# Block 2, first layer: two modulation rows moved from the first attention pairs to the front of the key-value projection

## The reference

```python
mod_x = (jax.nn.silu(c) @ w_mod[i] + b_mod[i])[:, None, :]
mod_c = (jax.nn.silu(c_ctx) @ w_mod[i] + b_mod[i])[None, None, :]
sh1, sc1, ga1, sh2, sc2, ga2 = jnp.split(mod_x, 6, axis=-1)
...
hx = rmsnorm_2(x, g_pre_mix[i]) * (1.0 + sc1) + sh1
px = hx @ w_in[i]
...
mix_x = jnp.concatenate([attn_x, four_x, hy_x], axis=-1) @ w_out[i]
x = x + ga1 * rmsnorm_2(mix_x, g_post_mix[i])
```

## Time and profile before

| what | value |
|---|---|
| median of 3 runs | 1646.79 us (1645.38 to 1646.94) |
| the profiled execution | 1647.11 us, its span 1645.3 us |
| TensorE busy | 1591.5 us |
| VectorE (DVE) busy | 1107.7 us |
| ScalarE (ACT) busy | 833.4 us |
| granted TensorE clock, mean | 0.996 of full speed |
| loads from memory | 259.12 MB |

### The profile page before, as it was taken

How to read it: one execution, slowest core, us unless ns; L and a number is a source line. 1 busy time by engine, 2 the same in 40 slices (tenths; PEclk the granted TensorE clock), 3 DMA queues, 4 the chain that set the end, 5 groups by cost and what they waited for, 6 DMA issues and landing times. The chain is left out here.

```text
span 1645.3 us, 22529 instructions
## 1 busy us (share of the span) xinstructions
PE 1591.5 (97%) x8474; PEld 1277.2 (78%) x8474; DVE 1107.7 (67%) x1822; ACT 833.4 (51%) x1524; POOL 265.1 (16%) x321
## 2 busy tenths in 40 slices
PE   8999999999999999999999999999999998899998
PEld 7667888787677888878846788888788786678886
DVE  5686899556867998655775654445433577589974
ACT  5555667445656666442354543333421544566653
POOL 2000011810003112700000001101272000001163
PEclk9999999999999999999999999999999999999999
DMA  8555866555579654551197433333232342356652
GB/s 275 174 190 168 227 184 183 191 183 178 194 240 264 170 158 151 205 179 63 73 318 246 129 103 102 103 87 92 103 128 87 107 133 91 92 148 184 187 188 86
DMA packets 267277, 261.72 MB, mean 159 GB/s; under 512 B 8965, under 2 KB 208937, under 8 KB 266530
## 3 DMA queue, kind: packets, MB, share of 16 engines
q1 hardware_dynamic: 262994, 246.15, 48.7%
q0 software_dynamic: 3888, 13.81, 2.4%
q10 hardware_dynamic: 288, 0.33, 0.1%
HBM read 259.12 MB, written 1.13 MB: 158 GB/s over the span
## 5 line engine op out<-in xcount | busy, mean ns | idle before, releaser
L578 PE MATMUL psv<-hHL,wH 128*128 128x512 f32 (+1 forms) x1952 | 639.1, 390 | 2.9 <-DVE wL L1286 2.9
L1286 DVE TENSOR_TENSOR wL<-ring,wH 128x1024 fp32r<-128x1024 f32 (+2 forms) x364 | 450.8, 1241 | 234.9 <-ACT wH L1969 231.7
L1969 ACT ACTIVATE wH<-ring 128x1024 fp32r<-128x1024 f32 (+2 forms) x364 | 377.2, 1040 | 274.4 <-PE psv L578 265.9
L578 PE MATMUL psv<-hHL,wL 128*128 128x256 f32 (+1 forms) x1504 | 465.1, 309 | 0.0
L578 PEld LDWEIGHTS psv<-hHL,wH 128*128 128x128 f32 x1952 | 363.3, 188 | 86.6 <-DVE wL L1286 6.4
L578 PE MATMUL psv<-wH,hHL 128*128 128x512 f32 (+2 forms) x936 | 318.0, 389 | 10.7 <-DVE hHL L1553 4.7
L578 PEld LDWEIGHTS psv<-hHL,wL 128*128 128x128 f32 x1504 | 283.6, 189 | 15.7
L578 PE MATMUL pss<-wH,hHL 128*128 128x512 f32 (+3 forms) x808 | 272.0, 381 | 0.0
L578 PEld LDWEIGHTS psv<-wH,hHL 128*128 128x128 f32 x936 | 175.7, 189 | 53.3 <-DVE wL L1286 9.5
L578 PE MATMUL psv<-wL,hHL 128*128 128x512 f32 (+2 forms) x468 | 179.9, 384 | 0.0
L1101 POOL TENSOR_TENSOR W<-scr 128x256 f32<-128x256 f32 (+1 forms) x88 | 82.4, 937 | 582.3 <-ACT scr L2178 582.3
(11 more groups left out here) (270 smaller groups left out, 1602.0 us busy)
## 6 DMA issues: line engine op xcount, KB each, us to landing
ring<-in_w_up SPq DMA_DIRECT2D x176, 512.0 KB, 5.1
ring<-in_w_mod SPq DMA_DIRECT2D x96, 512.0 KB, 5.0
ring<-in_w_down SPq DMA_DIRECT2D x88, 512.0 KB, 4.2
ring<-in_w_in SPq DMA_DIRECT2D x52, 512.0 KB, 4.7
ring<-in_w_out SPq DMA_DIRECT2D x32, 512.0 KB, 4.8
ring<-in_w_in SPq DMA_DIRECT2D x8, 384.0 KB, 5.7
W<-gate_scratch POOLq DMA_DIRECT2D x3, 1024.0 KB, 5.0
ring<-in_w_in SPq DMA_DIRECT2D x8, 288.0 KB, 6.9
```

The costliest lines, as they stand in the source:

```text
L578: return pe.matmul(o, a, b, start=start, stop=stop, skip_group_check=True)
L1286: v.tensor_tensor(lo, raw, hi.bitcast(F32), ALU.subtract).then_inc(piece_split, told("piece_split", p))
L1969: return ac.activation(o, i, ACT.Copy)
```

## The change

Rows 1 and 2 of the second layer's modulation leave the table `pairs` and stand in a new entry `between`; the entry `heads`, empty before, goes. The other seven rows of the table are spread on pairs 0, 2, 3, 5, 6, 8 and 10. On TensorE and on DVE row 1 now comes behind the gate transpose and row 2 behind the second forward transform's step; in the ring the four chunks stand between the query chunks and the key-value chunks.

```diff
-        MOD2 = [{"start": [0], "heads": [], "pairs": {0: 1, 1: 2, 2: 3, 3: 4, 5: 5, 6: 6, 7: 7, 9: 9, 10: 11}, "ffn": [8], "end": [10]},
-                {"start": [], "heads": [], "pairs": {}, "ffn": [], "end": []}]
+        MOD2 = [{"start": [0], "between": [1, 2], "pairs": {0: 3, 2: 4, 3: 5, 5: 6, 6: 7, 8: 9, 10: 11}, "ffn": [8], "end": [10]},
+                {"start": [], "between": [], "pairs": {}, "ffn": [], "end": []}]
...
             add_cols(A["w_in_2"][l], 0, 512, ph, "q")
+            add_mod(1, MOD2[l]["between"])
             add_cols(A["w_in_2"][l], 512, 512, ph, "kvf")
             add_raw(A["w_fourier_2"][l], 0, FOW)
-            add_mod(1, MOD2[l]["heads"])
             add_mod(1, MOD2[l]["pairs"].values())
...
                 transposes("V", (ph, "gates"), [(rowc[:, :], slice(0, P))])
+                for c in MOD2[l]["between"][0:1]:
+                    modulation_row(1, c)
                 hyena_back(0)
                 if not last:
                     hyena_forward(1)
+                for c in MOD2[l]["between"][1:]:
+                    modulation_row(1, c)
                 project_split(range(4), [512] * nt + [256] * (4 - nt), (ph, "kvf"))
...
-                modulation(1, MOD2[l]["heads"])
...
                 take_rows(96, ph, "gates")
+                for c in MOD2[l]["between"][0:1]:
+                    modulation_row(1, c)
                 hyena_gate(0)
                 if not last:
                     hyena_products(1)
+                for c in MOD2[l]["between"][1:]:
+                    modulation_row(1, c)
                 splits_to(first_piece[ph, "kvf"] + 2, 0)
...
-                modulation(1, MOD2[l]["heads"])
```

## The result

The changed kernel takes **1653.55 us** (median of 4 runs, 1651.83 to 1654.99), the kernel before 1646.37 us beside it (4 runs, 1645.38 to 1646.94): ratio 1.0044, 95% interval 1.0033 to 1.0056. It is slower by more than 0.2%, and the time lies 1.25 us above the range of the prediction. A second measurement (12 runs of it, 32 of the kernel before) gave 1651.42 against 1646.24 us: ratio 1.0034, interval 1.0021 to 1.0046. The intervals overlap, from 1.0033 to 1.0046. By the second ratio the cost is 5.6 us, which puts the changed kernel at 1652.4 us, just above the range; so the sign of the result is firm, and its distance from the range is not.

What follows compares the result with a forecast made beforehand. TensorE, busy for 97% of the span, was taken as the bound. New idle 2.83 plus moved work 3.72 less 4.33 saved in attention gave +2.2 us on 1646.8: 1649.0 us, range 1646.8 to 1652.3.

Steps and rivals of the forecast that it cites:

- The look-ahead: Ahead of the key-value projection: DVE's low halves follow row 2's addition, PE idles 2.8 us, the projection starts 6.55 us later.
- The chunk in time: Ahead of the key-value projection: the weight chunk lands in 4.1 us, at 788.6, with 4.4 us in hand.
- Pair 1: In attention, without a row: 5.29 us instead of 6.80, with PE idle 3.14 us until ACT's exponentials are done.
- What the attention gives back: From pair 1's to pair 11's scores: 50.32 us becomes 45.99, a saving of 4.33 us.
- 2.83 + 3.72 - 4.33: New idle ahead of the projection plus moved row work less the attention's saving: +2.2 us.
- the clock falls in one of the new gaps: Rival: half clock after the projection's or pair 1's gap; 1650.7 us with one fall (chance 0.30), 1652.3 with two (0.08).
- one gap of 2.66 us: PE's wait in pair 1 of the kernel before: matmuls after it showed no clock fall.
- between 2.66 and 3.00 us: The idle time on PE from which the clock was taken to fall; the new gaps were 2.8 and 3.14 us.
- The price of one fall: Eight transposes and four score matmuls at 1.2 GHz after a gap: 1.65 us more, paid in full.
- late weights: Rival: the key-value chunk lands late, PE waits ahead of the projection; 1649.8 us, or 1652.8 with 1 MB more; chance 0.08.
- pair 1 like pair 4: Rival, in attention: pair 1 takes 3.48 us in place of 5.29, time 1647.2 us; chance 0.08.
- the untouched look-ahead: Rival: low halves still come ahead of the row, the projection's 2.83 us idle vanishes, time 1646.2 us; chance 0.03.

Runs made afterwards that it cites:

- look-ahead cut: The kernel before, no row moved, with VectorE's and ScalarE's preparing ahead stopped before the key-value pieces: ratio 1.0037.
- chunks behind: The changed kernel with the four row chunks after the key-value chunks in the ring and row 2 after the projection: 1648.29 us, ratio 1.0012.
- filler in pair 1: The changed kernel with seven idle-filling matmuls in the gap ahead of pair 2's scores: 1648.92 us, ratio 1.0014.
- Both fillers: The changed kernel with six idle-filling matmuls ahead of the key-value projection and seven ahead of pair 2's scores: 1649.25 us, ratio 1.0008.
- Fourier late: The changed kernel with VectorE's four Fourier additions one attention step later: ratio 1.0024.
- both moves: The changed kernel with row chunks after the key-value chunks, row 2 after the projection and Fourier additions one step later: ratios 0.9998 and 0.9997.

## Why the prediction was wrong

**Right, by the profile.**
- *The look-ahead.* The low halves stand behind row 2's addition, and PE idles until the first is done. Forecast: the projection 6.55 us later; with row 1's start as the zero point it is 6.86 (13.69 less 6.83). The difference of 0.3 us is small: the first transform takes 0.10 us more behind a row, and a projection matmul that follows the transform directly is listed 0.27 us earlier than a row in its place (3.27 against 3.54 us behind the transform's start). The kernel with only the look-ahead cut shows that this, and not the chunk's arrival, is the cause.
- *The chunk in time.* ACT started on it at 790.71, where I had 788.6, with a landing of 6.3 us and not 4.1. 4.4 us of slack took that in. My row came from a load with nothing beside it; here two chunks and the gate load were on their way together. The Trainium skill, "DMA: Bandwidth & Descriptors", section "Bandwidth", gives 6.15 us of the DMA engines' time for 1 MB. By the prediction's estimate from that page, with the fixed cost and the gate load added, the chunk would have been in at 798.3; the trace doesn't agree, since ACT had it at 790.71, 7.6 us earlier.
- *Pair 1.* The idle of 3.14 us released by ACT's exponential is the forecast to the hundredth, and the four Fourier additions are 1.33 us of it.
- *What the attention gives back.* 4.33 us forecast. From pair 0's scores to the output projection it is 63.09 less 58.76 = 4.33 us, in two of the fillers' kernels and in the one with the chunks behind, none of which has a fall there. (The fillers' kernels are the one with the filler in pair 1 and the one with both.)

**The sum without a fall** is thus 6.86 - 0.11 - 4.33 = 2.4 us, where I had 2.2. Both fillers together, which leave just this, measured 1.0008 (0.9995 to 1.0021), 1.3 us.

**The step that failed** is the clock. The sum, 2.83 + 3.72 - 4.33, has no term for it, because I took "no fall" as the likeliest case; the first rival, "the clock falls in one of the new gaps", had 0.30 for one fall and 0.08 for both, and the range ended at the price of two. The profiled execution of the changed kernel has both falls, and they cost 1.50 us (37.77 less 36.27) and 1.57 us (60.33 less 58.76). In the profiles of kernels that have the gaps, the 2.61 us gap was followed by a fall in two of four and the 3.14 us gap in three of four.

Two reasons failed with it. That one gap of 2.66 us had no fall in the trace was a single reading of something that varies from one execution to the next. And the length of the gap, "between 2.66 and 3.00 us", doesn't decide: falls came behind 2.61, 1.81 and 0.99 us as well, and not always behind 3.14. The price of one fall, 1.65 us, was right in most cases: 1.50 and 1.44 ahead of pair 0 (37.77 and 37.71 less 36.27), 1.57, 2.63 and 1.41 behind pair 1's gap (60.33, 61.39 and 60.17 less 58.76).

By these frequencies, an estimate from few profiles, the change costs 2.4 + 0.5 x 1.5 + 0.75 x 1.9 = 4.6 us, ratio 1.0028. That lies inside the second measurement's interval and below the first's. A range that ends at 1652.3 also left out falls away from the change: the 1.47 us behind the stretch are of that kind, with the transforms at 1387 and the value products at 1399 at half clock in the one profile and not in the other. That the first measurement came out above the range is in part their doing, and so in part bad luck.

The rivals of late weights, of pair 1 like pair 4 and of the untouched look-ahead are excluded by the lists above.

**Open.** What decides whether the clock falls behind a given gap isn't settled. Nor is it settled why the first measurement's ratio, 7.2 us, is above 4.6. Its profiled execution is accounted for: 2.4 us without a fall, 3.1 for the two falls, and 1.7 outside the stretch. Whether its other three runs were alike isn't shown, and with four runs chance may be all there is to it.

## What to carry to other kernels

Where weights are prepared ahead by a rule with borders, look at what a moved load does to the borders before you count its bytes: here a border without any moved work cost as much as the whole change. A new idle time on a full TensorE is to be priced at its length plus the chance of a fall times its price (1.4 to 2.6 us here), and that chance can't be read from one profile. With two such gaps, followed by a fall in two of four and three of four profiles, "no fall" was not the likeliest case. And when runs spread by 0.5%, read the few stretches that the change touches: where no fall lay in them they agreed to 0.02 us, between executions whose totals differed by more than the effect. Look at what stands right behind them, too: a gain inside can be lost there.

## What was not expected of the hardware

**The clock.** Whether it falls does not follow from the length of the gap alone. In thirteen profiles: behind 0.99 us at this layer's output projection three of thirteen, behind 1.81 us (pair 1, Fourier late) one of four, behind 2.61 us two of four, behind 3.14 us three of four, behind 3.86 us one of one; behind 2.66 us, in the kernel before, none of one. Three waits of 0.80 to 0.99 us stand within 6 us there, and the falls come behind the last of them. Behind the 3.00 us near 1388 us, the four score matmuls took 2.08 us in all thirteen. There PE comes from transforms with other idle times, 1.94 us among them, shortly ahead; whether idle times close together are the reason was not tried. The Trainium skill, "TensorE: Matmul & The Clock Gate", section "HAM oscillation", names a length of idle time to stay under, and the gaps up to 3.14 us here do stay under it; the falls behind 0.99, 1.81, 2.61 and 3.14 us show that this is no protection in this kernel.

**Two paces at full clock.** The same instructions ahead of the change end up to 4.5 us apart from execution to execution (gates' transpose at 778.08 and at 782.59 us). The falls near 137, 432 and 530 us are only a part of it: two profiles have none of them (Fourier late, look-ahead cut), and their gates' transposes come at 778.71 and 781.30 us. The other part is a difference in pace at a granted clock of 1.00. Late in the kernel, from PE's wait for DVE near 1447 us to the one near 1578 us, nine profiles take 131.13 or 131.14 us and four take 128.80 or 128.81. Nothing lies between. In these window rows the count behind PE's busy time is of matmul records that fit into the same 110 us, first in the kernel before (a slower one), then with both fillers (a faster one):

```profile
1460.00:1570.00 110.00, 110.00 (x624) 95.44 (x623) 102.88 (x157) 77.83 (x138) 14.30 (x19) 1.00 0.66 189
```

```profile
1460.00:1570.00 110.00, 110.00 (x636) 96.97 (x635) 104.66 (x160) 79.92 (x141) 14.96 (x20) 1.00 0.67 190
```

Between 136 and 292 us there are again two values, 152.9 and 155.2 us where no fall lies in them. The two profiles of "both moves", one and the same kernel, have 155.22 and 152.91 there, so the pace is not set by the kernel. What sets it was not tried. Such a step of 2.3 us is as large as the forecast for the whole change, and it can be seen only because the stretches were read one by one.
